# Low half of the normalised activations and the shared region placed 64 bytes off the high half, modulo 2048

## The reference

```python
h = _rmsnorm(h_res, ln1_g[layer]);  proj = h @ w_in[layer]
...
h_res = h_res + jnp.square(jax.nn.relu(h2 @ w_ff1[layer])) @ w_ff2[layer]
...
def swiglu(x, w_in, w_out):
    a, b = jnp.split(x @ w_in, 2, axis=-1)
    return (jax.nn.silu(a) * b) @ w_out
```

## Time and profile before

| | |
|---|---|
| Time, median of 3 runs | 3246.8 us (3246.36 to 3249.54) |
| Span of the profiled execution | 3230.1 us; its own time is not listed, the median lies 16.7 us above the span |
| TensorE matmuls | busy 3136.0 us, 97% of the span, 18046 matmuls |
| TensorE weight loads | busy 2660.2 us, 82% |
| DVE, ACT, GpSimd | 53%, 39%, 60% |
| HBM | 426.95 MB read, 135 GB/s over the span |

### The profile page before, as it was taken

One profiled execution on the slowest core, in us unless ns is written; L12 is line 12 of the kernel. 1 busy time (PEld: TensorE's weight loads), 2 busy tenths in 40 slices (PEclk: granted clock), 3 DMA queues, 4 the chain that ended last, 5 costly groups with the idle time before them and its releaser, 6 DMA issues.

```text
span 3230.1 us, 48616 instructions
## 1 busy us (share of the span) xinstructions
PE 3136.0 (97%) x18046; PEld 2660.2 (82%) x18046; DVE 1724.8 (53%) x2409; ACT 1270.9 (39%) x2132; POOL 1950.4 (60%) x1285
## 2 busy tenths in 40 slices
PE   7999899999999999999999999999999999999998
PEld 6677899976779998888887777888888888886898
DVE  5665776655668865443435465544435443436554
ACT  4445555343555643222232443322223222235443
POOL 6658477514994975677567658678875777603000
PEclk9999999999999999999999999999999999999999
DMA  5323455632335663333443223334433443332354
GB/s 195 111 92 105 138 189 194 204 105 95 112 117 168 215 210 121 122 126 122 134 130 117 85 85 108 119 129 130 136 125 110 133 138 125 123 119 76 131 182 156
DMA packets 120280, 430.35 MB, mean 133 GB/s; under 512 B 13857, under 2 KB 17185, under 8 KB 119729
## 3 DMA queue, kind: packets, MB, share of 16 engines
q1 hardware_dynamic: 93632, 335.24, 31.7%
q0 software_dynamic: 24576, 86.46, 8.4%
q10 hardware_dynamic: 1904, 6.36, 0.5%
HBM read 426.95 MB, written 8.85 MB: 135 GB/s over the span
## 4 chain that ended last, share of the span: by engine, by line
PE 86%; POOL 5%; DVE 3%; ACT 2%; DMA 2%; issue 2%; ACTq 0%; DVEq 0%; SPq 0%; POOLq 0%
PE ps L484 22%; PE ps L486 21%; PE ps L485 21%; PE ps L511 2%; PE ps L581 2%; PE ps L582 2%; PE ps L583 2%; POOL macc L402 2%; DMA raw<-in_panels 2%; POOL modraw L400 2%; POOL mprod L400 1%; PE ps L525 1%; PE ps L530 1%; PE ps L526 1%; PE ps L986 1%
## 5 line engine op out<-in xcount | busy, mean ns | idle before, releaser
L1642 DVE TENSOR_TENSOR wlo<-raw,whi 128x1024 fp32r<-128x1024 f32 x632 | 856.0, 1355 | 914.6 <-ACT whi L1078 889.5
L1078 ACT ACTIVATE whi<-raw 128x1024 fp32r<-128x1024 f32 x632 | 668.4, 1058 | 1417.2 <-PE ps L486 901.2
L484 PE MATMUL ps<-xhi,whi 128*128 128x512 f32 (+2 forms) x2792 | 949.3, 340 | 3.1 <-DVE wlo L1642 2.5
L486 PE MATMUL ps<-xhi,wlo 128*128 128x512 f32 (+2 forms) x2792 | 934.6, 335 | 0.0
L485 PE MATMUL ps<-xlo,whi 128*128 128x512 f32 (+2 forms) x2792 | 933.7, 334 | 0.0
L484 PEld LDWEIGHTS ps<-xhi,whi 128*128 128x128 f32 x2792 | 531.8, 190 | 70.8 <-issue 14.8
L485 PEld LDWEIGHTS ps<-xlo,whi 128*128 128x128 f32 x2792 | 531.8, 190 | 51.8 <-issue 1.9
L486 PEld LDWEIGHTS ps<-xhi,wlo 128*128 128x128 f32 x2792 | 531.4, 190 | 50.2
L400 POOL TENSOR_SCALAR modraw<-modraw,cs 128x512 f32<-128x512 f32 x288 | 552.1, 1917 | 27.6
L400 POOL TENSOR_SCALAR macc<-modraw,cs 128x512 f32<-128x512 f32 x36 | 70.5, 1958 | 745.2 <-PE ps L511 602.5
L400 POOL TENSOR_SCALAR mprod<-modraw,cs 128x512 f32<-128x512 f32 x252 | 445.8, 1769 | 19.0 <-POOL macc L402 0.2
(11 more groups left out here) (362 smaller groups left out, 4752.9 us busy)
## 6 DMA issues: line engine op xcount, KB each, us to landing
raw<-in_panels SPq DMA_DIRECT2D x632, 512.0 KB, 3.3
modraw<-in_mod POOLq DMA_DIRECT2D x144, 512.0 KB, 4.4
bias_by_column<-in_rpb POOLq DMA_DIRECT2D x16, 476.2 KB, 8.3
bia<-bias_by_column POOLq DMA_DIRECT2D x32, 96.0 KB, 2.6
rtab<-in_rtab ACTq DMA_DIRECT2D x2, 1312.0 KB, 7.4
wuq<-in_wuq ACTq DMA_DIRECT2D x2, 768.0 KB, 6.7
con<-in_con SPq DMA_DIRECT2D x1, 1345.5 KB, 13.7
h<-in_x SPq DMA_DIRECT2D x1, 1088.0 KB, 6.7
```

What stands on the lines that cost most here:

```text
L484: pe.matmul(out, w_hi, x_hi, start=start, stop=False)
L486: return pe.matmul(out, w_lo, x_hi, start=False, stop=stop)
L1078: act.activation(whi[:, s * PW:(s + 1) * PW], raw[:, s * PW:(s + 1) * PW], ACT.Copy).then_inc(hi_split, 1)
L1642: dve.tensor_tensor(wlo[:, s * PW:(s + 1) * PW], raw[:, s * PW:(s + 1) * PW], whi[:, s * PW:(s + 1) * PW].bitcast(F32), ALU.subtract).then ...
```

## The change

`xlo` is taken from its place behind `xhi` and put right ahead of the shared region, behind the 64 bytes of `cs`, which move there too. `raw`, `whi` and all tensors up to `modv` move down by the 16384 bytes of `xlo`, so modulo 2048 they stay where they were (128). `xlo` now begins at 114880 and the shared region at 131264: both are 192 modulo 2048, while `xhi` (32896), `raw`/`wlo` (49280) and `whi` (65664) are 128. `gsc` and the region move up by 64 bytes; what lies behind `gsc` stays. `gates_l`, which borrows a piece of `xlo`, follows it. Every engine issues the same instructions in the same order as before, with other addresses.

```diff
         xhi_at = place[0]
-        xhi, xlo = sb("xhi", NC * T2, F32R), sb("xlo", NC * T2, F32R)
+        xhi = sb("xhi", NC * T2, F32R)
         raw_at = place[0]
...
         modv = sb("modv", DEPTH * MODT * 2)
+        cs = sb("cs", 2 * NC)
+        xlo_at = place[0]
+        xlo = sb("xlo", NC * T2, F32R)
         arena0 = place[0]
-        assert arena0 % 2048 == xhi_at % 2048, (arena0, xhi_at)
+        assert arena0 % 2048 == xlo_at % 2048 == xhi_at % 2048 + 64, (arena0, xlo_at, xhi_at)
         place[0] += 4 * AW
         gsc = sb("gsc", DEPTH * 3 * NC * 2)
-        cs = sb("cs", 2 * NC)
...
-        gates_l = nc.alloc_sbuf_tensor_at("gates_l", [P, T1], F32, offset=xhi_at + 4 * (NC * T2 + NC * T1))
+        gates_l = nc.alloc_sbuf_tensor_at("gates_l", [P, T1], F32, offset=xlo_at + 4 * NC * T1)
```

## The result

The change made the kernel slower: 3266.8 us, the median of 6 runs (3260.6 to 3274.1), against 3247.0 us for 6 runs of the kernel before beside them (3237.2 to 3249.5). The two medians are 19.8 us apart. The ratio is 1.0084, with a 95% interval of 1.0067 to 1.0101, so 22 to 33 us are lost; against the 3239.9 us of 23 further runs of the kernel before, beside the first experiments, the loss is 26.9 us. One of those 23, of 3882.7 us at a granted clock of 0.745, is left out of the ratios. The forecast was 3236.9 us, and 3254 us was the upper end of its range.

What follows compares the result with a forecast made beforehand. TensorE's start-to-start matmul distance was taken as the bound; 5.9 us (region) + 3.6 (`xlo`) + 0.4 (`token_quarter`) = 9.9 us off the 3230.1 us span gave 3220.2, plus 16.7 to the median: 3236.9 us, range 3222 to 3254 us.

Steps and rivals of the forecast that it cites:

- What bounds the kernel: Second block: time is the distance between TensorE matmul starts, matmuls busy 97% of the span; the change acts through addresses.
- Modulo 256, moving less weight: All split products: moving tile's address less weight tile's, modulo 256, sets the distance; assumed the right measure.
- the price for 512 columns: Shared region: 2688 products gain 2.2 ns each, 5.9 us, whatever the columns; excess means distance beyond the columns' own time.
- relation 0: Moving and weight tile addresses equal modulo 256, as for every second-block product before; 120.0 ns with 256 columns, 226.7 with 512.
- relation 64: Moving tile's address 64 beyond the weight tile's, modulo 256; where the change puts the region's products, forecast 2.2 ns less each.
- `xlo` moves, `xhi` does not: Second block: 1648 products of high weights by `xlo` gain 3.6 us at 2.2 ns; neighbours up to 7.3 us more.
- The first block: Stride 1088 runs through all four address relations as before: no change, with 2.0 us on either side for `xlo`.
- From span to time: Whole kernel: median lies 16.7 us above the profiled span; the same distance was added to the forecast span of 3220.2 us.
- Slower by switches: Rival on second-block `x`: 3296 switches between high and low at up to 4 ns, 13.2 us; 3254.1 us, chance 0.18.
- No change: Rival: the excess is fixed and the first block's 1.7 ns come from its stride; 3246.8 us, chance 0.23.
- what the prediction drew from a rule: All TensorE products: read ports shared with nobody, so operand column addresses do not matter; sum 0, 3246.8 us.
- The much faster case: Rival: relation 64 cuts the excess to 2.5 ns for 4528 products, 48.9 us; 3197.9 us, chance 0.07.

Runs made afterwards that it cites:

- the first experiments: Against the kernel before: shared region alone moved by 64 bytes, ratio 1.0006; `xlo` alone, 1.0061; `xhi`, `xlo` and region all at 192 modulo 2048, 1.0033.
- the series: Four separate kernels without the reference's work: rows of 72 products on TensorE alone, offsets varied; 512 columns took 226.7 ns at offset 0, 228.9 ns at 64.
- the version with a relation for each stage: Against the kernel before: second-block stages with 256 columns moved by 64, first-block `xlo` 64 off `xhi`, 512-column stages unmoved; 3230.0 us, ratio 0.9979.
- the first kernel of series: Separate kernel, 72 products a case, moving areas at offsets 0 to 224 from the weights' place; 256 columns took 120.0 ns at 0, 113.3 ns at 64.
- the third: Separate kernel, 72 products a case, with 128, 96, 64 or 32 weight columns loaded; 512 columns at offset 0 took 226.7 ns with 128, 231.7 with 32.
- the kernel with everything at 64: Against the kernel before: `xhi`, `xlo` and the shared region all at 192 modulo 2048, weights at 128; 3252.7 us, ratio 1.0033.

## Why the prediction was wrong, step by step

**What bounds the kernel** was right: TensorE's start-to-start distance in the second block, which the change acts on through addresses alone.

**Modulo 256, moving less weight** was right for 512 columns. Offsets of 256, 512 and 1024 give the distance of 0, and weights moved by 192 give that of moving areas moved by 64, both with 512 columns; with 256 columns the same relation was met at two distances (below). The forecast of 117.8 ns for `ghi` with 256 columns, worked out as a mean over the other three relations, was met (117.9 ns) by luck: the other relations are far from equal when each is kept for good (113.3 to 118.7 ns in the series), and their mean doesn't give the distance of a stride that runs through them.

**The step that failed** is the price for 512 columns: "I take 2.2 and not 0.6, because the excess is the same 13.3 ns for 256 and 512 columns, so the price belongs to the weight load's time and not to the columns". That excess is the same only at relation 0. At relation 64 it is 15.6 ns with 512 columns (228.9 ns) and 11.1 or 6.6 ns with 256 (117.8 or 113.3 ns); and with 512 columns it does not follow the number of weights loaded. The 656 groups of `ghi` and `rhi` with 512 columns were booked as a gain of 2.2 ns a product and lose 2.2 ns: 4.3 us lost in place of 4.3 us gained. Of the forecast's 9.9 us only the part with 256 columns of the region came, 1.6 us. (The 126.7 ns that the forecast assumed for 272 columns at relation 0, from the same excess, measure 125.3 ns in the series.)

**`xlo` moves, `xhi` does not** was the largest miss in microseconds. The text booked 3.6 us of gain on one product of three and left the two neighbours open, "from no change to 2.2 ns each", a gain only. On average all three lose 5.2 ns with 512 columns, 20.0 us; with 256 columns nothing came of it (120.0 ns), and `token_quarter`, booked as a gain of 0.4 us, lost 2.3 us. `xlo` moved alone shows it without the region, and high and low moved together bring it down to 2.2 ns.

**The first block** came out at nothing, as forecast, for another reason. `x` gained in the steady stretches (126.3 to 125.0 ns with 272 columns), but in the profiled executions the same 8118 matmuls start within 1225 us: TensorE is busy 2.3 us less there (1166.68 and 1169.00 us) and idle as much more, so that the gain was given back to waits. In the version with a relation for each stage 8150 start in that stretch. The rows are those of before and of that version:

```profile
0.00:1225.00 1225.00, 1169.00 (x8118) 1004.41 (x8118) 797.23 (x1262) 608.94 (x1201) 804.79 (x517) 0.97 0.46 151
...
0.00:1225.00 1225.00, 1166.05 (x8150) 1004.33 (x8150) 802.27 (x1275) 611.37 (x1205) 802.48 (x517) 0.97 0.45 151
```

With `xlo` alone moved, which puts the first block's activations in the same relations as the change and this version do, 7983 start, at a granted clock of 0.96. So one profile of each doesn't settle what the first block gains.

**From span to time.** The 16.7 us put between span and median were no fixed part: the profiled execution of after took 3260.6 us for a span of 3258.8 us, and in the other executions, too, the time is 1.8 us above the span. By that the profiled execution of before took some 3231.9 us, an estimate, 15 us less than the median that the forecast added back: the rest is the spread of executions.

**The rivals.** Slower by switches was right in its sign and its place, `x`, and named the observation that would show it ("if `ghi` gains and `x` loses"). Its price, up to 4 ns a switch for all forms, was too low and not general: with 512 columns the mixture costs 4.5 ns a product, 13.5 ns for the two switches of a group of three, at another offset of the low half nothing (192 in the series), and with 256 columns `x` didn't lose. Nor could the rows that it was read from carry it: 0.13 and 0.12 us there are times to the nearest 10 ns. It also lacked that relation 64 costs at 512 columns without any switch. No change is excluded, and with it what the prediction drew from a rule. The Trainium skill, page "SBUF — State Buffer", section "Who interferes with whom", has TensorE wait for nobody. By that the same products would stand equally far apart at every offset; with every other engine idle they are 226.7, 228.9 and 233.3 ns apart, and the measurement decides. Whether it is a read that waits is not shown. The much faster case, an excess of 2.5 ns, was found nowhere with 512 columns; of plain float32, from which it was drawn, the series shows that it has that excess at each of the offsets tried (0, 64 and 128).

**What stays open.** Why 512 columns run best at relation 0 and 256 columns worst near it, what the mixture does at 512 columns, and why one address pattern can settle at two distances. The last is seen in several places, all with 256 columns: at relation 64 they take 113.3 ns in the series and 117.8 ns at 320, which is the same modulo 256; at 192 they take 113.3 ns in the first kernel of series and 117.8 ns in the third; in the kernel with everything at 64, `ghi` takes 117.8 ns and `nhi` 113.4 ns; and `x` with 256 columns, relations 0, 64, 0, takes 120.0 ns in the changed kernel and 117.7 ns with `xlo` moved alone, at the same addresses modulo 2048. That the weight load and the moving operand meet in the memory is a reading that fits the part of the address difference; it was not shown, since neither a wider step of the weights nor fewer weight columns took the excess away with 512 columns.

## What to carry to other kernels

A price per instruction read from one tile size holds for that size: before it is booked, it is measured at the size that most of the time is in, here by a series of 72 equal products, which took one short kernel and would have given the sign. Where float32r products follow one another with a weight load each, the two operands' address difference modulo 256 is worth a scan for every column count, and with 512 columns high and low halves with different ones can cost more than either alone (232.0 ns against 226.7 and 228.9 ns), which another pair doesn't (228.9 ns against 226.7 and 233.3 ns). Different stages can have different best places, and aliases into the same room give each its own.

## What the runs showed of the hardware that was not expected

- At the 2.4 GHz level, float32r products with a weight load each start 226.7 to 234.3 ns apart with 512 columns and 113.3 to 120.0 ns apart with 256, where only the offsets differ (weight columns 4 bytes apart). With 512 columns the address difference decides; with 256 the same difference can give 113.3 or 117.8 ns. Above the columns' own time (213.3 and 106.7 ns) the most frequent values lie near 6.7, 13.3 and 20.0 ns.
- Plain float32 products with 512 columns take 429.1 ns a pass at offsets 0, 64 and 128, and 256 columns take 215.8 ns, so 256 more columns cost 213.3 ns, two clocks each at 2.4 GHz, with 2.4 to 2.5 ns over: no effect of the address.
- Fewer loaded weight columns can make a product slower: 226.7 ns with 128 and 231.7 ns with 32, at 512 moving columns and offset 0.
- With 192, 224 and 240 moving columns the products start 111.3 to 111.8 ns apart, at offsets 0 and 64 alike, though their columns take 80, 93 and 100 ns.
